# The first recurrence group of mixer 2 four steps later, and ScalarE's work for a group cut in three parts

## The reference

```python
xa = depthwise_conv(u_a, conv_a_w[l], conv_a_b[l], LRU_CONV // 2)
r = jax.nn.sigmoid(block_diag(xc, wa, ba)); i = jax.nn.sigmoid(block_diag(xc, wx, bx))
log_a = -LRU_C * r * jax.nn.softplus(-lam)
a = jnp.exp(log_a)
b_in = jnp.sqrt(-jnp.expm1(2.0 * log_a)) * (i * x32)
_, h = lax.associative_scan(_lin_combine, (a, b_in), axis=1, reverse=reverse)
y_a = (h_fwd + h_bwd) @ p_a[l]
merged = gates[..., :D_MODEL] * y_a + gates[..., D_MODEL:] * y_b
```

## Time and profile before

| | us |
|---|---|
| median of 3 runs | 1912.34 |
| lowest, highest | 1910.85, 1914.88 |
| the profiled execution | 1913.9 |
| its span | 1912.2 |
| TensorE busy in the span | 1868.7 |
| VectorE busy | 1237.5 |
| ScalarE busy | 535.4 |
| GpSimd busy | 46.4 |

### The profile page before, as it was taken

How to read it: one execution, slowest core, us unless ns; L and a number is a source line. 1 busy time by engine, 2 the same in 40 slices (tenths; PEclk the granted TensorE clock), 3 DMA queues, 4 the chain that set the end, 5 groups by cost and what they waited for, 6 DMA issues and landing times.

```text
span 1912.2 us, 21585 instructions
## 1 busy us (share of the span) xinstructions
PE 1868.7 (98%) x8628; PEld 1491.8 (78%) x8628; DVE 1237.5 (65%) x1658; ACT 535.4 (28%) x492; POOL 46.4 (2%) x67
## 2 busy tenths in 40 slices
PE   8999999999999999999999999989999999999997
PEld 6888888778878778888888888866678888788875
DVE  6764567757745487443344779958875788736874
ACT  4333222132332222221221111248851122112210
POOL 0000000000000000000000000012200000000000
PEclk9999999999999999999999999999999999999998
DMA  5224341473111332222222224232214322223221
GB/s 189 99 77 141 116 161 63 130 258 122 67 67 45 110 132 82 94 92 89 105 88 85 91 96 147 68 108 88 69 57 147 113 88 88 82 93 110 80 69 71
DMA packets 48133, 195.04 MB, mean 102 GB/s; under 512 B 6720, under 2 KB 15168, under 8 KB 33344
## 3 DMA queue, kind: packets, MB, share of 16 engines
q1 hardware_dynamic: 48064, 194.10, 29.6%
HBM read 181.23 MB, written 12.85 MB: 101 GB/s over the span
## 4 chain that ended last, share of the span: by engine, by line
PE 68%; issue 20%; DVE 9%; ACT 1%; DMA 0%; SPq 0%; DVEq 0%; POOLq 0%; POOL 0%; ACTq 0%
PE bank L915 21%; PE bank L917 21%; PE bank L916 21%; DVE wlo L1255 2%; PE xb L1180 2%; DVE squares L1709 0%; PE xb L1126 0%; DVE win L1638 0%; DMA raw<-in_up 0%; PE bank L1022 0%; PE xb L1116 0%; PE bank L1023 0%; PE bank L1024 0%; PE xb L1134 0%; ACT whi L641 0%
## 5 line engine op out<-in xcount | busy, mean ns | idle before, releaser
L915 PE MATMUL bank<-uhi,whi 128*128 128x512 f32 x1560 | 627.3, 402 | 11.0 <-DVE wlo L2082 7.0
L917 PE MATMUL bank<-uhi,wlo 128*128 128x512 f32 x1560 | 621.1, 398 | 0.0
L916 PE MATMUL bank<-ulo,whi 128*128 128x512 f32 x1560 | 621.1, 398 | 0.0
L641 ACT ACTIVATE whi<-raw 128x2048 fp32r<-128x2048 f32 (+3 forms) x178 | 301.0, 1691 | 1083.6 <-PE bank L917 1049.2
L1255 DVE TENSOR_TENSOR wlo<-raw,whi 128x2048 fp32r<-128x2048 f32 (+3 forms) x178 | 358.9, 2016 | 89.0 <-ACT whi L641 86.2
L915 PEld LDWEIGHTS bank<-uhi,whi 128*128 128x128 f32 x1560 | 295.7, 190 | 84.8 <-issue 9.7
L917 PEld LDWEIGHTS bank<-uhi,wlo 128*128 128x128 f32 x1560 | 295.6, 189 | 72.1
L916 PEld LDWEIGHTS bank<-ulo,whi 128*128 128x128 f32 x1560 | 295.8, 190 | 71.6 <-issue 1.4
L915 PE MATMUL bank<-hhi,whi 128*128 128x512 f32 x528 | 210.2, 398 | 4.4 <-DVE hlo L1308 4.4
L917 PE MATMUL bank<-hhi,wlo 128*128 128x512 f32 x528 | 210.0, 398 | 0.0
L916 PE MATMUL bank<-hlo,whi 128*128 128x512 f32 x528 | 210.0, 398 | 0.0
(11 more groups left out here) (387 smaller groups left out, 1852.1 us busy)
## 6 DMA issues: line engine op xcount, KB each, us to landing
raw<-in_up SPq DMA_DIRECT2D x65, 1024.0 KB, 4.8
raw<-in_win SPq DMA_DIRECT2D x16, 1024.0 KB, 4.8
raw<-in_wout SPq DMA_DIRECT2D x8, 1024.0 KB, 4.8
raw<-in_down1a SPq DMA_DIRECT2D x8, 768.0 KB, 4.4
tab<-tab_kept SPq DMA_DIRECT2D x4, 1536.0 KB, 8.5
raw<-in_down2a SPq DMA_DIRECT2D x8, 768.0 KB, 4.3
raw<-in_down3a SPq DMA_DIRECT2D x8, 768.0 KB, 4.2
raw<-in_down1b SPq DMA_DIRECT2D x8, 640.0 KB, 4.1
```

The costliest lines, as they stand in the source:

```text
L641: act.activation(whi[s][:, 0:width], raw[s][:, 0:width], ACT.Copy).then_inc(w_hi, 1)
L915: pe.matmul(dst, wh, hi, start=first, stop=False)
L916: pe.matmul(dst, wh, lo, start=False, stop=False)
L917: return pe.matmul(dst, wl, hi, start=False, stop=last)
```

## The change

`HEAD_FIRST` goes from 4 to 8. The groups on TensorE then lie at (13, 0), (13, 6), (14, 5), (15, 3), (16, 2), (17, 0), (17, 7), (18, 5), (19, 4) and (20, 2).

ScalarE's functions of a group become three parts: sigmoids and tanh (`lru_gate_parts`), the root of the group before (`lru_roots`), and the exponentials (`lru_powers`). Casts may lie between the parts. Where they lie is worked out from `unit_begins` and `gates_end`, in k steps with 2.5 for each group, with the offsets `LRU_PARTS`. The gate sigmoids are held back and made just before the next sigmoids of a group. From unit 13 on, ScalarE's order is (S sigmoids and tanh, R root, E exponentials): cast 13, cast 14, gate sigmoids 12, S0, E0, S1, cast 15, R0, E1, gate sigmoids 13, S2, cast 16, R1, E2, S3, R2, cast 17, E3, S4, R3, cast 18, E4, S5, R4, E5, S6, cast 19, R5, E6, S7, cast 20, R6, E7, gate sigmoids 18, S8, cast 21, R7, E8, gate sigmoids 19, S9, R8, cast 22, E9, gate sigmoids 20, R9, cast 23, gate sigmoids 21, cast 24, and so on.

VectorE's order becomes: output 12, variance 0, output 13, scan 0, variance 1, output 14, scan 1, variance 2, output 15, scan 2, variance 3, scan 3, output 16, variance 4, scan 4, variance 5, output 17, scan 5, variance 6, output 18, scan 6, variance 7, output 19, scan 7, variance 8, output 20, scan 8, variance 9, output 21, scan 9.

SP's code is the same, but it places the loads of `wg` by `head_slot`. No instruction of arithmetic is added or removed.

```diff
-HEAD_EVERY, HEAD_FIRST, HEAD_LATE, SIDE_LATE = 6.5, 4, 6, 3
+HEAD_EVERY, HEAD_FIRST, GATES_TAKE = 6.5, 8, 2.5
+LRU_PARTS = (0, 4, 6, 8)
+
+def head_step(h):
+    return HEAD_FIRST + int(HEAD_EVERY * h)
 
+def unit_begins(i):
+    at = KD * (i - M2["wp"][0] - 1)
+    return at + GATES_TAKE * sum(head_step(h) < at for h in range(HEADS))
+
+def gates_end(h):
+    return head_step(h) + GATES_TAKE * (h + 1)
...
-                for i in range(M2_UNITS):
-                    high(nb + i, 0, A[M2_KIND[i][0] + "2"].shape[-1])
-                    for h in range(HEADS):
-                        if head_turn(h) == i:
-                            lru_functions(h)
-                            if h == HEADS - 1:
-                                lru_roots(h)
-                    if i >= 2 and M2_KIND[i - 2][0] in ("ga", "gb"):
-                        gates(*M2_KIND[i - 2])
+                units, sigmoids = list(range(M2_UNITS)), []
+
+                def highs(until, alone=False):
+                    while units and unit_begins(units[0] - 1) <= until:
+                        i = units.pop(0)
+                        high(nb + i, 0, A[M2_KIND[i][0] + "2"].shape[-1])
+                        if i >= 2 and M2_KIND[i - 2][0] in ("ga", "gb"):
+                            sigmoids.append(M2_KIND[i - 2])
+                            if alone:
+                                waiting_gates()
+
+                def waiting_gates():
+                    while sigmoids:
+                        gates(*sigmoids.pop(0))
+
+                highs(gates_end(0) + LRU_PARTS[0], True)
+                for h in range(HEADS):
+                    highs(gates_end(h) + LRU_PARTS[0])
+                    waiting_gates()
+                    lru_gate_parts(h)
+                    highs(gates_end(h) + LRU_PARTS[1])
+                    if h:
+                        lru_roots(h - 1)
+                    highs(gates_end(h) + LRU_PARTS[2])
+                    lru_powers(h)
+                highs(gates_end(HEADS - 1) + LRU_PARTS[3])
+                waiting_gates()
+                lru_roots(HEADS - 1)
+                highs(KD * M2_UNITS * 2, True)
...
-                    while units and KD * (units[0] - M2["wp"][0]) <= until:
+                    while units and unit_begins(units[0] + 1) <= until:
...
                 for h in range(HEADS):
-                    side_units(HEAD_FIRST + int(HEAD_EVERY * h))
+                    side_units(gates_end(h) + LRU_PARTS[3])
                     lru_variance(h)
-                    side_units(HEAD_FIRST + int(HEAD_EVERY * (h + 1)) + SIDE_LATE)
+                    side_units(gates_end(h) + HEAD_EVERY + GATES_TAKE + LRU_PARTS[2])
                     lru_scans(h)
```

More of the change, by code:

```diff
@@ L61 @@
 M2_KIND = {i: (name, u) for name, at in M2.items() for u, i in enumerate(at)}
-HEAD_EVERY, HEAD_FIRST, HEAD_LATE, SIDE_LATE = 6.5, 4, 6, 3
+HEAD_EVERY, HEAD_FIRST, GATES_TAKE = 6.5, 8, 2.5
+LRU_PARTS = (0, 4, 6, 8)
+def head_step(h):
+    return HEAD_FIRST + int(HEAD_EVERY * h)
 def head_slot(h):
-    at = HEAD_FIRST + int(HEAD_EVERY * h)
+    at = head_step(h)
     return M2["wp"][0] + 1 + at // KD, at % KD
+def unit_begins(i):
[3 more added lines that the diff above has]
+    return head_step(h) + GATES_TAKE * (h + 1)
 class Tally:
@@ L121, in rolled_on @@
         t.base, t.local, t.turn = t.base + (end - start - 1) * t.per, 0, None
-def head_turn(h):
-    i, k = head_slot(h)
-    return i + 1 + (k >= HEAD_LATE)
 def columns(names_widths):
@@ L785, in gates, with lru_gate_parts @@
                     last.then_inc(gate2_ready, 1)
-                def lru_functions(h):
+                def lru_gate_parts(h):
                     q = h % 2
@@ L806, in lru_functions, with lru_powers @@
                         act.activation(lru_v[:, q, d, :], ut[:, d, :], ACT.Tanh, scale=lam[:, 0, c:c + 1])
-                    if h:
-                        lru_roots(h - 1)
+                def lru_powers(h):
+                    q = h % 2
                     for d in range(2):
@@ L1780, in mixer2 @@
                 for h in range(HEADS):
-                    side_units(HEAD_FIRST + int(HEAD_EVERY * h))
+                    side_units(gates_end(h) + LRU_PARTS[3])
                     lru_variance(h)
-                    side_units(HEAD_FIRST + int(HEAD_EVERY * (h + 1)) + SIDE_LATE)
+                    side_units(gates_end(h) + HEAD_EVERY + GATES_TAKE + LRU_PARTS[2])
                     lru_scans(h)
-                side_units(KD * M2_UNITS)
+                side_units(KD * M2_UNITS * 2)
                 for u in range(KD):
```

## The result

| | kernel before | kernel after |
|---|---|---|
| median of 20 runs each, side by side, us | 1913.69 (1909.01 to 1917.13) | 1907.82 (1903.37 to 1912.08) |
| ratio after / before, 95% interval | | 0.9971 [0.9963, 0.9978] |
| span of the first profiled execution, us | 1912.2 | 1903.9 |
| predicted, us | | 1910.3 (1905.5 to 1914.5) |

The changed kernel is faster by 0.29%: 5.9 us by the medians, 4.2 to 7.1 by the interval. The time lies in the range of the prediction, but the predicted gain was 2.0 us, and most of the chance (0.62) lay on a difference within 0.2%. The direction was right and the size too small.

What follows compares the result with a forecast made beforehand. TensorE is 98% busy; 7.8 us go, but the recurrence chain on ScalarE and VectorE sets the end, returning 10.9 us idle and 2.4 us clock. 1913.9 less 2.0 is 1911.9, on the median's scale 1910.3 us (1905.5 to 1914.5).

Steps and rivals of the forecast that it cites:

- The first wait: TensorE before group 0: the pool wait and its clock loss go, 7.8 us in all; group 0 still starts at 1264.3.
- Units 13 to 21 without a break: Sign of being right: TensorE runs these units without a wait, its only long one coming in unit 22.
- The chain: Recurrence on ScalarE and VectorE: nine periods, 122.3 us in all; tenth scan starts at 1411.7 instead of 1413.99.
- All seven meetings: GpSimd's products of groups 3 to 9 overlap VectorE instructions in periods 2 to 8, costing 1.9 to 2.4 us each.
- The wait at the end: TensorE in the last step of unit 22 idles 10.9 us for group 9's output; sign named 10 to 12 us.
- the 1408 that was to show me wrong: Sign of being wrong: a scan of group 9 on VectorE that starts before 1408.
- The clock at the restart: TensorE after the wait in unit 22: low clock costs 2.4 us, between nothing and twice 2.1 us.
- The price for the casts: If VectorE's casts also wait for GpSimd's product, the tenth scan ends 0.9 us later and the gain is 1.1 us.
- what is late next: Unit 22's last step waits for the recurrence chain, which starts no earlier: 10.9 us idle, unit 23 at 1420.4.
- Rival 1: VectorE's meetings with GpSimd don't come: 1906 us with half gone, 1902.5 with all gone; chance 0.26.
- Rival 2: The three remaining GpSimd products also meet VectorE, 2.3 us each: tenth output 6.9 us later, 1917.2 us; chance 0.11.
- rival 3: TensorE's two long waits with their clock, 13.2 us, vanish and nothing comes back: 1899 us; chance 0.03.

Runs made afterwards that it cites:

- step_only: The kernel before with only the first group's step moved (`HEAD_FIRST` 4 to 8), helper engines' orders unchanged: 1922.11 us, ratio 1.0050 to the kernel before.
- parts_only: The kernel after with the first group's step set back (`HEAD_FIRST` 8 to 4): 1912.46 us, ratio 1.0001 to the kernel before.
- before_look1: The kernel before, unchanged, profiled a second time: its single execution took 1911.56 us.
- after_again: The kernel after, unchanged, run again beside the kernel before: 1906.11 us, ratio 0.9969 to the kernel before.
- no_product: The kernel after without GpSimd's product (input gate not multiplied by `xa`): 1901.26 us, ratio 0.9945 to the kernel before.
- product_after_variance: The kernel after with GpSimd's product held back until VectorE's variance of that group is done: 1902.55 us, ratio 0.9957 to the kernel before.

## Why the prediction was right in its mechanism and short in its size

**The first wait.** Right: group 0 starts 11.4 us behind unit 12 without a wait; 7.8 us go.

**Units 13 to 21 without a break.** Right: no wait of TensorE there in three traces of the kernel after.

**The chain.** The first scan's product starts 36.4 us behind unit 12's start (36.5 foreseen). The nine periods are 13.2, 15.3, 11.3, 15.0, 13.5, 13.6, 13.5, 13.9 and 11.8 us, each within 0.4 of the forecast; their sum is 121.1 instead of 122.3, and the tenth scan comes 1.3 us earlier behind unit 12's start than I had it. All seven meetings came, with the products of groups 3 to 9, at a mean of 2.1 us (six variance instructions of 3.28 to 3.42 us instead of 1.22, and `ya_lo` of 2.77 instead of 0.69), where I had 1.9 to 2.4: 14.7 us for 15.5. That is 0.8 of the 1.3 us. Most of the rest lies in the waits for ScalarE, which were 1.42, 1.80, 1.16 and 1.15 us in front of low halves and 1.19 and 1.20 in front of scans, where I had 1.5, 1.9, 1.2, 1.2, 1.3 and 1.3.

**The wait at the end.** 9.5 us in the last step of unit 22, put down to `ya_lo`; I had 10.9. By the letter of my signs this is below the 10 to 12 us that I named, and the tenth scan's product starts at 1407.72, before the 1408 that was to show me wrong. But unit 12 starts 2.6 us earlier in this execution than in the one that I read; on that one's clock the product starts at 1410.4.

**The clock at the restart.** I took 2.4 us between bounds of nothing and 4.2. Three traces show 1.6, 1.5 and 2.6, mean 1.9.

**The price for the casts.** The rule did not come to bear: no cast falls beside a product in the changed order (ten casts, 4.3 us). In step_only two do, and take 2.46 and 2.47 us instead of 0.43, and in parts_only three. So a cast waits as well. The Trainium skill, SBUF — State Buffer, section SBUF: two separate sides, has an instruction in a two-port mode take the port pair as one with two SBUF inputs does, and counts an fp32 copy within SBUF among the former; by that rule, these rows agree, though no run shows in which mode the cast is. In the order of this change it altered nothing.

**The sum.** In the stretch the predicted gain is 2.0 us; the chain gave 1.3 more and the clock 0.5, 3.8 in all. The measured gain there is 4.05; the remaining 0.25 us is no more than three traces of one kernel differ by (183.9 to 184.3). The step that failed is the term "what is late next": its shape was right and it was 1.3 us too dear, and the term for the clock 0.5 us. Each is small, but the margin of the forecast was only about 2 us, the difference of 15.6 us lost before and 13.4 us lost after, so these two errors doubled the gain in the stretch. That the time fell into the range owes something to luck: 1.35 us of the error in the gain are hidden by the slower kernel before, and some 1.8 us of the measured gain come from no term of the sum.

**What stays open.** The stretch gives 4.05 us, the medians 5.9 (4.2 to 7.1). In the first pair of traces the span is 8.3 us shorter: 4.3 in the stretch, 1.1 in the start-up and twice 1.55 us (less 0.2 at the end) in two passages through norms, near 1120 and near 1660, where the code is unchanged. Those passages are long where the granted clock falls there. The windows of the kernel after, and below of the kernel before:

```profile
1120.00:1125.00 5.00, 5.00 (x25) 4.15 (x25) 1.78 (x10) 0.00 (x0) 1.64 (x1) 1.00 0.01 3
```

```profile
1120.00:1125.00 5.00, 5.00 (x24) 4.33 (x24) 1.35 (x9) 0.00 (x0) 1.64 (x1) 0.66 0.21 85
```

They come and go: the passage at 1120 is short in two of three traces of the kernel after and in one of three of the kernel before, the one at 1660 in three of three and in one of three. A third one near 1840 is long in before_look1 and after_again, by 1.5 us, with a granted clock of 0.66 from 1842 to 1847 in both. So each trace of the kernel before has one or two such losses, in all five, and the traces of the kernel after have none, two and none. Among the experiments both kinds occur with either order. With three traces each this can't be told from chance. Whether the change makes these falls rarer, or the remaining 1.8 us is only the scatter of the medians, was not settled.

**The rivals.** Rival 1 (meetings that don't come) was not what happened, but it names what can still be had: with the product behind the variance the meetings shrink and the time falls to 1902.55. That this is my 1902.5 for no meetings at all is luck: I had the tenth output 7.2 us earlier without them, and no_product shows 6.0, from a time 2.5 us below my forecast, and ends at 1901.26. Rival 2 (ten meetings) and rival 3 (no loss) did not occur.

## What to carry to other kernels

When a wait in front of a chain is removed but the chain starts no earlier, its idle time is collected at the chain's end; the gain is the difference of two large terms, so state its own range, and step the orders of all engines to find it. Moving a step and recasting the helper engines' order belong together: here one half alone costs 9.4 us and the other gives nothing. When an instruction is longer than its siblings of the same form and names no releaser, look at what GpSimd does at that moment, and put GpSimd's work beside instructions that read PSUM: here one added wait gave 4.3 us on top of the change's 5.9 (5.3 us in the stretch). In the old order, where VectorE waits for ScalarE anyway, the same added wait gave 1.3 us, which can't be told from nothing. Of the complete kernels of this study, product_after_variance (1902.55 us) is the fastest.

## What the runs showed of the hardware

- A VectorE cast of one input (128x512, 0.43 us) took 2.46 to 2.52 us beside a product of GpSimd (five of them, two in step_only and three in parts_only); VectorE's outputs that read PSUM kept their time beside it.
- The same 9.5 us wait of TensorE cost 1.5, 1.6 or 2.6 us at the clock of 0.50 (1.2 GHz) after it, in three executions of one kernel, and waits of 3.5, 3.6 and 6.3 us cost 2.6, 2.5 and 2.7 us in three others.
- A VectorE instruction with two inputs of 1.22 us (128x1024) took 3.28 to 3.42 us beside a product of GpSimd, and one of 0.69 us (128x512) took 2.77 us, with no idle time before it and no releaser in the profile.
- An unchanged passage of TensorE differs by 1.5 us between executions, with the granted clock of 0.66 or 1.00 in the same window.
